# Inverting the blocks for two chunks at a time, and subtracting decay times k'S from each chunk's values in place

## What is computed

```python
qkv = silu(causal_depthwise_conv(qkv, conv_w))           # 4 taps
q, k = l2_norm(q) * A_DK ** -0.5, l2_norm(k)
g = cumsum(g)                                             # log decay within the chunk
decay = exp(where(tri, g[:, None] - g[None, :], -inf))
lower = where(strict, beta[:, None] * (k @ k.T) * decay, 0)
u, w = solve(I + lower, [v * beta, k * beta * exp(g)])    # unit lower triangular
qk = (q @ k.T) * decay
def step(S, ...):
    v_new = u - w @ S
    o = (q * exp(g)) @ S + qk @ v_new
    S = S * exp(g_last) + (k * exp(g_last - g)).T @ v_new
o = rms_norm(o) * silu(z); x = x + o @ w_out
```

## Time and profile before

| | us |
|---|---|
| median of 3 runs | 1533.15 (1530.92 to 1533.5) |
| span of the profiled execution, first to last instruction | 1528.9 |
| PE busy in it | 1509.2 |
| DVE busy | 920.3 |
| ACT busy | 735.1 |
| GpSimd busy | 257.7 |

### The profile page before, as it was taken

How to read it: one execution, slowest core, us unless ns; L and a number is a source line. 1 busy time by engine, 2 the same in 40 slices (tenths; PEclk the granted TensorE clock), 3 DMA queues, 4 the chain that set the end, 5 groups by cost and what they waited for, 6 DMA issues and landing times.

```text
span 1528.9 us, 21108 instructions
## 1 busy us (share of the span) xinstructions
PE 1509.2 (99%) x7848; PEld 1211.0 (79%) x7848; DVE 920.3 (60%) x1733; ACT 735.1 (48%) x1284; POOL 257.7 (17%) x446
## 2 busy tenths in 40 slices
PE   9999999999999999999998999999999999999998
PEld 7878888888888877877876887666778888888887
DVE  5767777787654566677778445554475243433467
ACT  4454455544553346655667234566555241332343
POOL 2044334444312003433341000000000000000000
PEclk9999999999999999999999999999999999999999
DMA  5321111111114232222221231111222222222221
GB/s 207 110 70 51 61 56 56 56 56 56 45 57 152 97 112 89 84 71 73 87 84 55 101 107 64 56 69 56 69 89 104 87 98 107 93 100 95 99 83 69
DMA packets 40165, 127.25 MB, mean 83 GB/s; under 512 B 4576, under 2 KB 9104, under 8 KB 40064
## 3 DMA queue, kind: packets, MB, share of 16 engines
q1 hardware_dynamic: 38112, 121.65, 23.1%
q0 software_dynamic: 1040, 3.27, 0.6%
q10 hardware_dynamic: 912, 0.99, 0.2%
HBM read 122.69 MB, written 2.15 MB: 82 GB/s over the span
## 4 chain that ended last, share of the span: by engine, by line
PE 89%; ACT 5%; DVE 3%; issue 2%; DMA 0%; POOL 0%; SPq 0%; DVEq 0%; ACTq 0%; POOLq 0%
PE ps L884 87%; PE ps L1263 1%; PE ps L1029 1%; ACT wh L1407 1%; ACT L L1820 1%; DVE wl L2018 1%; ACT L1832 1%; ACT L1400 1%; DVE L L2560 1%; ACT L L1781 0%; ACT xreg L1832 0%; ACT sp L1914 0%; DVE up L2172 0%; ACT sp L1912 0%; ACT pT L1841 0%
## 5 line engine op out<-in xcount | busy, mean ns | idle before, releaser
L884 PE MATMUL ps<-xr,wh 128*128 128x512 f32 x2720 | 871.6, 401 | 1.8 <-DVE xr L2609 0.9
L884 PEld LDWEIGHTS ps<-xr,wh 128*128 128x128 f32 x2720 | 498.9, 188 | 123.6 <-issue 26.1
L884 PE MATMUL ps<-xr,wl 128*128 128x512 f32 x1376 | 537.6, 391 | 0.0
L2018 DVE TENSOR_TENSOR wl<-wraw,wh 128x1024 fp32r<-128x1024 f32 x214 | 261.5, 1230 | 134.2 <-ACT wh L1407 133.2
L884 PEld LDWEIGHTS ps<-xr,wl 128*128 128x128 f32 x1376 | 258.2, 188 | 55.8
L1407 ACT ACTIVATE wh<-wraw 128x1024 fp32r<-128x1024 f32 x214 | 222.0, 1048 | 74.4 <-PE ps L884 73.1
L884 PE MATMUL ps<-xm,wh 128*128 128x512 f32 x640 | 197.8, 390 | 0.0
L884 PEld LDWEIGHTS ps<-xm,wh 128*128 128x128 f32 x640 | 119.5, 188 | 26.2 <-DVE xm L2695 1.6
L884 PE MATMUL ps<-xm,wl 128*128 128x512 f32 x320 | 124.5, 389 | 0.0
L2869 POOL TENSOR_SCALAR L<-L,m 128x256 f32<-128x256 f32 (+1 forms) x120 | 90.6, 774 | 189.0 <-DVE m L2575 189.0
L2056 DVE SCALAR_TENSOR_TENSOR qkv<-cin,gains,qkv 128x512 f32<-128x512 f32 x96 | 85.5, 892 | 9.7 <-ACT qkv L1437 8.9
(11 more groups left out here) (283 smaller groups left out, 1773.2 us busy)
## 6 DMA issues: line engine op xcount, KB each, us to landing
wraw<-in_wa SPq DMA_DIRECT2D x48, 512.0 KB, 3.2
wraw<-in_wb SPq DMA_DIRECT2D x32, 512.0 KB, 3.8
wraw<-in_wu SPq DMA_DIRECT2D x32, 512.0 KB, 3.2
wraw<-in_wd SPq DMA_DIRECT2D x32, 512.0 KB, 3.2
wraw<-in_wao SPq DMA_DIRECT2D x16, 512.0 KB, 3.2
wraw<-in_wbo SPq DMA_DIRECT2D x16, 512.0 KB, 3.6
wraw<-in_wc SPq DMA_DIRECT2D x16, 512.0 KB, 3.3
bias<-rel_rows SPq DMA_DIRECT2D x16, 256.0 KB, 3.9
```

What stands on the lines that cost most here:

```text
L884: return e.matmul(out, w, x, start=start, stop=stop, skip_group_check=True)
L2018: e.tensor_tensor(m.wl[:, i % N_SPLIT, :], m.raw[:, i % N_RAW, :], m.wh[:, i % N_SPLIT, :].bitcast(F), ALU.subtract).then_inc(s.wlo, 1)
```

## The change

- In `levels` two chunks are handled as one: `AT` of chunks 2 and 3 is transposed on PE (`aT`, a new group in prep) and added by DVE to that of chunks 0 and 1 (`X`), so that one 128-wide matrix holds the lower blocks of one chunk and the upper ones of another. Masks of both halves are made once (three transposes, one addition). Each P and U group has two products of 128 columns instead of four of 64. One tile `W` holds the inverses and their transposes; DVE subtracts the result from W in place. For chunks 2 and 3 the inverse comes out transposed, so a last group `TF` turns those two.
- `w`, `kg` and `wT` are gone. For chunks 1 to 3 PE computes k'S (`k1`, `k2`, `k3`, with the tile `kc` for k), DVE subtracts decay times it from the chunk's values in place (`v1`, `v2`, `v3`), and r is the one product U'v. `recur` has 14 pieces instead of 11.
- The plans of rounds 2, 3 to 7, 8 and 9 are written anew.

```diff
 PLAN = {
-    "a": plan("p0 q2 q0 p4 q1 q0 p1 p0 q3 q2 p0 q1 p0 q2 p0 r2 r2 r0 p2 r0 p2 r1 p0 p2 r2 r1 r2 r1 p1 r2 p2 p2 r14"),
+    "a": plan("p0 q2 q0 p4 q1 q0 p1 p0 q3 q2 p0 q2 p0 q2 p0 r1 r2 r0 p2 r1 r0 p2 r1 r1 p0 r0 p2 r1 r2 r2 r1 p1 r2 p2 p2 r2"),
...
+    def sides(self, par, first, i, q, n):
+        v, c = self.W[:, par], 1 << i
+        base, step = {"turned": (0, 512 + c), "kept": (256 + c, 512 - c), "left": (256, 512 + c)}[first]
+        return bass.AP(v.tensor, v.offset + base + 128 * q, [list(v.ap[0]), [2 * c, 64 * n // c], [step, 2], [1, c]])
...
@@ tensor_program, prep
+        o = bank()
+        for q in range(2):
+            ins = e.transpose(o[:, q, :], m.AT[:, 2 + q, :], m.ident)
+        end(ins, (s.prep_v, prep_v(h, "X")))
...
@@ tensor_program, levels
-            for n in range(4):
-                ins = mm(o[:, n], m.Mm[:, i % 2, n, :], T[:, n])
+            for q in range(2):
+                T = m.sides(par, "turned", i, q, 1) if i < 6 else m.W[:, par, q].rearrange("p (b t c) -> p b t c", t=2, c=64)
+                ins = mm(m.sides_in(LEV_BANK, i, q, 1), m.Mm[:, i % 2, q, :], T)
...
-            for n in range(4):
-                ins = mm(o[:, n], m.Pm[:, n, :], V[:, n])
+            for q in range(2):
+                ins = mm(m.sides_in(LEV_BANK, i, q, 1), m.Pm[:, q, :], m.sides(par, "kept", i, q, 1))
...
-        end(four(bank(), lambda n: m.kg[:, n, :], lambda n: U[:, n, :]), (s.lev_a, lev_a(h, "w")))
+        o = bank()
+        for q in range(2):
+            ins = e.transpose(o[:, q, :], m.W[:, par, 6 + q, :], m.ident)
+        end(ins, (s.lev_a, lev_a(h, "TF")))
...
@@ tensor_program, recur
-            ins = mm(m.banks[4][:, 0:256], m.U[:, par, n, :], m.vt[:, par, n, :], True, n == 0)
-            if n:
-                e.wait_ge(s.rec_v, REC_V * h + n)
-                ins = mm(m.banks[4][:, 0:256], m.wT[:, par, n, :], so, False, True)
-            ins.then_inc(s.rec_p, 1)
+            if n == 0:
+                e.wait_ge(s.lev_v, lev_v(h, "U6"))
+                e.wait_ge(s.prep_a, prep_a(h, "v1"))
+            else:
+                if n == 2:
+                    e.wait_ge(s.lev_a, lev_a(h, "TF"))
+                e.wait_ge(s.rec_v, rec_v(h, f"S{n}"))
+                mm(m.banks[4][:, 256:512], m.kc[:, par, ts], so).then_inc(s.rec_p, 1)
+                yield
+                e.wait_ge(s.rec_v, rec_v(h, f"v{n}"))
+            mm(m.banks[4][:, 0:256], m.U[:, par, n, :], m.vt[:, par, n, :]).then_inc(s.rec_p, 1)
...
@@ vector_program, prep
-        did(e.tensor_tensor(k, k, m.rq[:, 0, :], ALU.mult))
+        did(e.tensor_tensor(m.kc[:, par, :], k, m.rq[:, 0, :], ALU.mult))
...
-        did(e.tensor_tensor(m.kg[:], o, bc(m.egn[:, col]), ALU.mult))
...
+        did(e.tensor_tensor(m.X[:], o[:, 0:2, :], m.AT[:, 0:2, :], ALU.add))
...
@@ vector_program, levels
+            V = m.sides(par, "kept", i, 0, 2)
+            did(e.tensor_tensor(V, V, m.sides_in(LEV_BANK, i, 0, 2), ALU.subtract))
...
@@ vector_program, recur
         for n in range(4):
+            if n:
+                v = m.vt[:, h % 2, n, :]
+                e.wait_ge(s.rec_p, rec_p(h, f"k{n}"))
+                did(e.scalar_tensor_tensor(out=v, in0=m.banks[4][:, 256:512], scalar=m.egn[:, 4 * h + n:4 * h + n + 1],
+                                           in1=v, op0=ALU.mult, op1=ALU.add))
+                yield
...
@@ pool_program, prep
-            masked(m.Mm[:, i % 2], m.masks[:, i, :]).then_inc(s.lev_o, 1)
+            masked(m.Mm[:, i % 2], m.X[:], m.masks[:, i, :]).then_inc(s.lev_o, 1)
```

More of the change, by code:

```diff
@@ L753, in __init__ @@
         self.za = new("za_silu")
-        self.m16, self.unit, self.upper, self.rows16, self.inv = (
-            new(n) for n in ("block_mask", "block_unit", "upper_halves", "block_rows", "block_inverse"))
+        self.m16, self.unit, self.rows16, self.inv = (
+            new(n) for n in ("block_mask", "block_unit", "block_rows", "block_inverse"))
+        self.both = new("both_halves")
         self.ohi, self.olo = new("o_hi"), new("o_lo")
@@ L844, in lev_o, with rec_p, rec_v @@
     return len(LEV_O) * h + LEV_O[name]
+def rec_p(h, name):
+    return len(REC_P) * h + REC_P[name]
+def rec_v(h, name):
+    return len(REC_V) * h + REC_V[name]
 def stick_p(j, name):
@@ L1070, in prep @@
             yield
-        yield from idle(5)
+        o = bank()
+        for q in range(2):
+            ins = e.transpose(o[:, q, :], m.AT[:, 2 + q, :], m.ident)
+        end(ins, (s.prep_v, prep_v(h, "X")))
+        if h == 0:
+            e.wait_ge(s.masks, 16)
+            cleared(LEV_BANK)
+            for i in range(4, 7):
+                ins = e.transpose(m.bk(LEV_BANK)[:, i - 4, :], m.masks[:, i, :], m.ident)
+            ins.then_inc(s.both, 1)
+            clear[LEV_BANK] = [(s.both, 2)]
+        yield
+        yield from idle(4)
     @part
     def levels(h):
-        U = m.U[:, h % 2]
+        par = h % 2
         def bank():
@@ L1625, in levels @@
                 e.wait_ge(s.lev_p, lev_p(h - 1, "U6"))
-            else:
-                e.wait_ge(s.unit, 5)
-            did(e.activation(m.half(m.Pm[:], i, 0), m.halves_in(LEV_BANK, i), ACT.Copy))
+            did(e.activation(m.Pm[:], o, ACT.Copy))
             yield
@@ L1632, in levels @@
                 e.wait_ge(s.lev_p, lev_p(h, "T5"))
-                did(e.activation(m.half(m.Tm[:], 6, 0), m.half(o, 6, 0), ACT.Copy))
+                b = m.banks[LEV_BANK][:]
+                x = bass.AP(b.tensor, b.offset, [list(b.ap[0]), [128, 2], [320, 2], [1, 64]])
+                did(e.activation(m.W[:, par, 0:2, :].rearrange("p q (t c) -> p q t c", t=2), x, ACT.Copy))
                 yield
-        e.wait_ge(s.lev_p, lev_p(h, "w"))
-        if h >= 2:
-            e.wait_ge(s.rec_p, REC_P * (h - 2) + 11)
-        did(e.activation(m.wT[:, h % 2], o, ACT.Copy))
+        e.wait_ge(s.lev_p, lev_p(h, "TF"))
+        did(e.activation(m.W[:, par, 4:6, :], o, ACT.Copy))
         yield
@@ L2362, in prep @@
                 yield
+        o = product("aT")
+        if h:
+            e.wait_ge(s.lev_o, lev_o(h - 1, "M6"))
+        did(e.tensor_tensor(m.X[:], o[:, 0:2, :], m.AT[:, 0:2, :], ALU.add))
+        if h == 0:
+            e.wait_ge(s.both, 1)
+            e.tensor_tensor(m.masks[:, 4:7, :], m.masks[:, 4:7, :], m.bk(LEV_BANK)[:, 0:3, :], ALU.add).then_inc(s.both, 1)
         e.wait_ge(s.prep_a, prep_a(h, "eb"))
@@ L2780, in begin, with masked @@
         e.tensor_scalar(m.const(C_EPS2), eps, eps, 128.0, ALU.mult, ALU.mult).then_inc(s.unit, 1)
-        e.memset(m.Pm[:], 0.0).then_inc(s.unit, 1)
-    def masked(out, mask):
-        return e.tensor_tensor(out, m.AT[:], mask.unsqueeze(1).to_broadcast([128, 4, 128]), ALU.mult)
+    def masked(out, x, mask):
+        n = x.shape[1]
+        return e.tensor_tensor(out, x, mask.unsqueeze(1).to_broadcast([128, n, 128]), ALU.mult)
     @part
```

128 lines of the change are left out of this document (61 added, 67 removed).

## The result

The changed kernel takes 1551.68 us (median of 4 runs, 1550.26 to 1551.79), the kernel before on the same chip 1533.33: ratio 1.0126 (95% interval 1.0112 to 1.014), slower by 18 to 19 us. The profiled execution spans 1548.3 us, 19.4 more than the earlier trace rows, both at a mean granted clock of 1.000. The direction was forecast, the size was not: 1541 was said, and 1549 was the upper end of the range.

What follows compares the result with a forecast made beforehand. PE was taken as the bound, busy 1509.2 of 1528.9 us. Per steady head, 5.25 us of waits against 3.1 saved and 0.3 of today gave +1.8; all rounds +8, span 1537, time 1541, 8-in-10 range 1525 to 1549.

Steps and rivals of the forecast that it cites:

- What PE is spared: PE's queue: halved passes in the levels and w replaced by transposes save 3.1 us a head, 25 us for eight.
- rival (4): A pass's price goes by columns, so merging 64-column products spares little: 1562 us, chance 0.02.
- The steady head's waits: Rounds 3 to 7: seven new PE waits, together 5.25 us a head, making each head 1.8 us longer.
- d0: Recurrence: d0 stands right behind r0 with no step to cover ACT's copy of r; wait 0.71 us.
- r3: Recurrence: r3 waits for v3, queued on DVE behind S3, taps, X, qd and wl; wait 1.9 us, 1.25 at least.
- sum: Norm's sum: three steps instead of four stand behind o3; wait 0.4 us.
- ks: Next head's ks waits for an ACT chain with the first tap ahead of ln and exp; wait 1.4 us.
- The chain behind o3: Late o3 leaves evacuation, tap, ln and exp no time to spare, so ks comes 7.7 us behind the sum's start.
- The other rounds by the same prices: Round 1 +0.5 us, round 2 +0.3, round 8 0, round 9 -2, priced as in the steady heads.
- From the span to the time: The median of the runs lies 4.2 us above the span, so span 1537 gives 1541 us.
- (2): Only waits the order forces are paid, 2.85 us a steady head; 1529 to 1535 us, chance 0.18.
- (3): DVE runs ahead and serves v3 in time, so waits are hidden: 1522, or 1508 with none; chance 0.18.

Runs made afterwards that it cites:

- run 1: Changed kernel with DVE's third update of v moved ahead of one conv tap, X and qd in rounds 3 to 7: 1545.27 us, ratio 1.0089.
- run 11: Changed kernel with X, qd and two conv taps moved behind the norm's additions on DVE in round 2: 1547.56 us, ratio 1.0105.
- Run 7: Changed kernel with the pieces reordered in rounds 1, 2, 8 and 9 alone: 1537.26 us, ratio 1.0045.
- run 2: Changed kernel with the step behind d0 and o0 moved ahead of them in rounds 3 to 7: 1566.72 us, ratio 1.023.
- run 4: Kernel before with only the recurrence in place and the changed kernel's order, inversion as before: 1564.0 us, ratio 1.0217.
- run 9: Kernel before with only other PLAN rows for rounds 1 to 9, sought in the same way: 1538.13 us, ratio 1.0056.
- runs 5 to 7 and 9: Changed kernel reordered in rounds 1 to 9 (1517.88 us), 3 to 7 alone (1530.56), 1, 2, 8, 9 alone (1537.26); kernel before reordered (1538.13).
- runs 4, 9 and 10: Kernel before with only the recurrence (1564.0 us); with only other PLAN rows (1538.13); with only the new inversion, reordered (1520.99).

## Why the prediction missed

For the steady heads, the mechanism and the sign were right. The step that failed is the sum for the other rounds. Step by step:

- **What PE is spared**: 3.1 us a head forecast. Distances of starts less gaps give 46.6 before and 43.5 after. Right, and rival (4) falls: the group of four 128-column passes above takes half of the earlier trace rows, not the same. The Trainium skill, "TensorE: Matmul & The Clock Gate", in its section on the back-to-back issue gap, has the gap of an isolated product grow with its columns, about 60 cycles up to 64 and 134 at 128. In these rows, of products that follow one another, a pass costs 0.11 us at both widths, and this case goes by them.
- **The steady head's waits**: 5.25 forecast, 5.34 measured (5.7 of gaps less the 0.36 of before). That the two are so close is luck in part, since the seven terms come to 4.3, none above its forecast. By term, as the distance of starts less the queue time: d0 0.71 and 0.64; d2 0.49 and 0.42; r1 0.25 and 0.13; r2 0.1 and nothing; r3 1.9 and 1.67; sum 0.4 and 0.39; ks 1.4 and 1.05; then, all of which I had at nothing, 0.2 ahead of the second product of level 5; 0.1 at each of five groups behind a wait, since the two passes behind a wait start 0.32 apart where they start 0.22 apart otherwise; and 0.3 that I can put down to no row. The head came to +2.2, not +1.8, for a slip: I took off the 0.3 us of before's own gaps as if the change removed them, and they are still there. That is nearly 2 us in five heads.
- **The chain behind o3**: the size of r3 was about right, and of ks too (7.47 us behind the sum, 7.7 forecast), with the tap ahead of ln as the cause; but that it counts because o3 is late was wrong (run 1). With ln at the 1.06 us of before, ks would still be due 7.0 us behind the sum against 6.4 of PE's work, so by these rows some 0.6 of the 1.05 comes from the one step less and the rest from the tap. That is an estimate; no run separates them.
- **The other rounds by the same prices** is the step that failed: -1.2 us forecast and +8.7 measured, which is 9.9 of the 11.7 us missing on the span (2.2 of it before round 2, 3.1 in round 2, 4.7 behind round 7). I had carried the recurrence's prices over to these rounds, and had followed the queues there only for k1 and o3. Missing were ks behind the bank of X in round 1 (1.3 us); in round 2 the k transposes behind DVE's kd (1.8) and the norm's sum behind X, qd and two taps (3.0, run 11); and in rounds 8 and 9 a number of short ones: 1.5 for the copy of r (458.74), 1.1 for kd (420.77), 0.9 and 0.6 for the state ahead of k'S, 0.7 for W. The one wait that I had followed in round 2, S1 behind the shuffles, came as forecast (1.1, forecast 1.2). But the terms that I named for that round sum to some -0.5, not to the +0.3 I took, and the upper end of the range was made of steady-head terms alone: nothing in it stood for these rounds. Run 7 shows that these are of the order's making: with other rows for those four rounds alone 12.7 us go, more than the 8.7 that the change had cost there.
- **From the span to the time**: the 4.2 us that I added is no fixed offset. In every execution that has both, the time is 1.8 to 2.1 us above the span; of the three executions before, only the one of 1530.92 fits the profiled span so, and the median was of the two longer ones. Like with like, 1537 was forecast for a span of 1548.3.
- **The rivals**: (2) and (3) did not come about in the order given. (3) is what the rewritten order comes near to, 1518 against the 1508 that all waits gone would give. (Its 1522, with r3 and ks at nothing, comes out of its own terms as 1525.)

Left open: why the sum takes 0.4 us more in run 1 (DVE's second addition there lasts 1.04 us in place of 0.69), and what the recurrence in place is worth by itself under a good order.

## What to carry to other kernels

On an engine that is full, work taken out counts only if the order around it still covers every chain; price the chains in each irregular round by following the queues, as in the regular one, for most of the miss was there. When a dependency gets a new link on a second engine, look first at what stands ahead of that link in its queue: twice here, moving three or four unrelated instructions behind it was worth 3 to 6 us with no other engine's order changed. And move cover only where the next link has some to spare: one step given to a wait of 0.6 us opened one of 3 us.

## What the runs showed of the hardware

TensorE's granted clock fell behind some gaps of 3 us and not behind others. Windows of run 2 (d0 behind the step), of the changed kernel and of run 1 (v3 first) (us, busy times, then PE's clock, DMA share, GB/s), each stretch right behind such a gap:
```profile
338.00:343.00 5.00, 5.00 (x19) 4.07 (x18) 2.61 (x13) 0.98 (x2) 2.57 (x8) 0.66 0.30 106
```
```profile
149.00:154.00 5.00, 4.68 (x19) 3.56 (x20) 2.18 (x4) 2.06 (x4) 0.00 (x0) 1.00 0.00 0
```
```profile
149.00:154.00 5.00, 4.80 (x12) 3.37 (x13) 1.37 (x3) 1.32 (x2) 0.00 (x0) 0.66 0.00 0
```
The mean of 0.66 is made of stretches at 1.00 and at the lower level, 1.2 GHz, and there the passes of 512 columns start 0.42 us apart (339.28 to 340.13 for two, in run 2) instead of 0.23. It cost 1.5 us in a head of run 2 (53.0 against 51.4), in three of its five, and 1.5 in round 2 of run 1, which is why that span fell by 4.2 and not by 5.8. The idle time ahead was 3.1 us in each of these. Other lengths went with a fall elsewhere: in run 4 it fell behind the sum's wait of 1.9 us of idle (149.47; the ones above show 3.0 of idle), and in the control (run 9) behind waits of 3.6 and of 1.4 us for Tm. A window behind the latter:
```profile
159.00:161.00 2.00, 2.00 (x9) 1.61 (x7) 1.81 (x3) 2.00 (x4) 1.25 (x1) 0.50 0.40 119
```
Why it fell behind some only, no run tells. A wait of 3.1 us can so cost half as much again as it lasts.

Executions of one kernel differ in this too. Of the 15 of the kernel before on the chip of runs 5 to 7 and 9, 13 took 1530.2 to 1530.7 us at a mean granted clock of 0.999 or 1.000, and two took 1533.7 and 1533.9 at 0.997. The changed kernel took 1550.26 at 1.000, and 1551.66 to 1551.79 at 0.999. So a difference of up to 3 us between two kernels can be the clock alone, as part of the ones in runs 4, 9 and 10 is.
